# A decoder trunk on one core: index scores in fewer places and ahead of the memory attention, the starting norms in thirds, other places for the top eights

## The reference, cut to what matters

```python
h = layer_norm(x, ln0_g, ln0_b)
for l in range(DEPTH):                       # DEPTH = 2
    pr = split_projection(h @ w_in[l])
    # A: sparse attention on the 128 keys that an index score picks
    logits = einsum('bqhd,bkd->bqhk', qi, ki)            # 8 index heads of 32
    score = einsum('bqhk,bqh->bqk', relu(logits), wi)    # causal, then top 128
    # B: block attention, C: difference of two softmaxes, then an RMS norm
    # D: latent attention, E: attention over 256 rows of mem
    mk, mv = mem @ w_mem_kv[l]
    o = stack(o_a, o_b, o_c, o_d, o_e) * silu(z)
    out = sum(sigmoid(g) * (o @ w_branch), branches) @ w_out[l]
    h = layer_norm(ALPHA * h + out, ln_g[l], ln_b[l])
```

## Time and profile before

| | us |
|---|---|
| median of 3 runs | 1339.69 (1339.42 to 1339.84) |
| profiled execution | 1343.1 |
| its span, first to last instruction | 1341.5 |
| PE busy / DVE / ACT / POOL in the span | 1307.1 / 707.8 / 662.8 / 663.4 |
| mean granted clock of PE | 0.995 |

### The profile page before, as it was taken

How to read it: one execution, slowest core, us unless ns; L and a number is a source line. 1 busy time by engine, 2 the same in 40 slices (tenths; PEclk the granted TensorE clock), 3 DMA queues, 4 the chain that set the end, 5 groups by cost and what they waited for, 6 DMA issues and landing times.

```text
span 1341.5 us, 18893 instructions
## 1 busy us (share of the span) xinstructions
PE 1307.1 (97%) x6744; PEld 1108.3 (83%) x6744; DVE 707.8 (53%) x1700; ACT 662.8 (49%) x1326; POOL 663.4 (49%) x838
## 2 busy tenths in 40 slices
PE   6999999999999999999999999999999999999996
PEld 5888888888888998888887888888888889888885
DVE  4746686554347464513355577675534664454135
ACT  3555445365477475523235552554646665654232
POOL 3443453354565454467435335434445553645774
PEclk8999999999999999999999999999999999999998
DMA  7322232132332143242413223322223213323321
GB/s 278 105 79 64 83 98 79 50 94 64 87 98 59 45 120 109 59 112 77 137 42 109 79 64 92 97 60 73 83 63 103 71 52 88 101 60 92 92 91 63
DMA packets 147053, 116.47 MB, mean 87 GB/s; under 512 B 5520, under 2 KB 131856, under 8 KB 146704
## 3 DMA queue, kind: packets, MB, share of 16 engines
q1 hardware_dynamic: 146816, 114.22, 28.9%
q10 hardware_dynamic: 144, 1.05, 0.2%
HBM read 112.10 MB, written 3.15 MB: 86 GB/s over the span
## 4 chain that ended last, share of the span: by engine, by line
PE 80%; DVE 12%; ACT 4%; issue 2%; DMA 1%; SPq 0%; DVEq 0%; ACTq 0%
PE product L811 19%; PE product L813 18%; PE product L812 18%; PE scores L1036 3%; PE context L1083 3%; PE transposed L1049 3%; PE branch_product L811 3%; PE branch_product L812 3%; PE branch_product L813 3%; PE context L1066 2%; ACT score_operands L1107 1%; DVE index_scores L1568 1%; PE product L911 1%; DVE top_eight L1574 1%; DMA merged<-in_w_mem_kv_dram 1%
## 5 line engine op out<-in xcount | busy, mean ns | idle before, releaser
L795 POOL TENSOR_TENSOR weights_rest<-raw_weights,weights_head 128x320 fp32r<-128x320 f32 (+3 forms) x672 | 542.5, 838 | 391.4 <-ACT weights_head L1107 391.2
L811 PE MATMUL product<-weights_head,stationary_head 128*128 128x512 f32 (+3 forms) x768 | 290.7, 379 | 3.0 <-issue 2.1
L813 PE MATMUL product<-weights_head,stationary_rest 128*128 128x512 f32 (+3 forms) x768 | 284.6, 371 | 0.0
L812 PE MATMUL product<-weights_rest,stationary_head 128*128 128x512 f32 (+3 forms) x768 | 284.5, 370 | 0.0
L1107 ACT ACTIVATE weights_head<-raw_weights 128x1280 fp32r<-128x1280 f32 (+4 forms) x178 | 197.7, 1113 | 142.1 <-PE product L813 116.5
L811 PE MATMUL product<-stationary_head,weights_head 128*128 128x512 f32 x640 | 260.4, 407 | 0.0
L813 PE MATMUL product<-stationary_head,weights_rest 128*128 128x512 f32 x640 | 250.4, 391 | 0.0
L812 PE MATMUL product<-stationary_rest,weights_head 128*128 128x512 f32 x640 | 250.3, 391 | 0.0
L780 POOL TENSOR_TENSOR merged<-merged,activated 128x256 f32<-128x256 f32 x128 | 94.0, 756 | 242.5 <-DVE activated L1712 242.5
L811 PEld LDWEIGHTS product<-weights_head,stationary_head 128*128 128x128 f32 x768 | 144.7, 188 | 25.5 <-issue 3.0
L813 PEld LDWEIGHTS product<-weights_head,stationary_rest 128*128 128x128 f32 x768 | 144.5, 188 | 23.8
(11 more groups left out here) (232 smaller groups left out, 1879.1 us busy)
## 6 DMA issues: line engine op xcount, KB each, us to landing
raw_weights<-in_w_in_dram SPq DMA_DIRECT2D x104, 512.0 KB, 3.7
raw_weights<-in_w_in_dram SPq DMA_DIRECT2D x72, 256.0 KB, 2.9
raw_weights<-in_w_branch_dram SPq DMA_DIRECT2D x80, 128.0 KB, 3.7
raw_weights<-in_w_out_dram SPq DMA_DIRECT2D x16, 512.0 KB, 3.7
merged<-in_w_mem_kv_dram SPq DMA_DIRECT2D x8, 512.0 KB, 7.2
raw_weights<-in_w_in_dram SPq DMA_DIRECT2D x8, 416.0 KB, 3.1
raw_weights<-in_w_in_dram SPq DMA_DIRECT2D x8, 296.0 KB, 4.6
residual<-in_x_dram SPq DMA_DIRECT2D x4, 512.0 KB, 11.5
```

The lines of the kernel that those rows point to most:

```text
L795: ins = nc.gpsimd.tensor_tensor(WL[:, sw, part], RAW[:, sr, part], WH[:, sw, part].bitcast(F32), ALU.subtract)
L811: nc.tensor.matmul(dst, sh, mh, start=start, stop=False)
L812: nc.tensor.matmul(dst, sh, ml, start=False, stop=False)
L813: return nc.tensor.matmul(dst, sl, mh, start=False, stop=stop)
```

## The change

Five things are changed.

1. The start of layer 0. `ln0` comes in three parts that are placed one by one. The loads of the memory weights come earlier and those of tiles 2 and 3 later. The copy of the transposed memory to DRAM is issued at `ek` and not at once. The first memory products wait for one quarter of the transposed memory at a time. `mv` stands ahead of `xj 1`. POOL's bias of tile t is written at its own gain and not one step later.
2. The IX groups. `xj 3` follows (IX,2,2) in place of (IX,2,1), group (IX,2,2) stands ahead of (IX,0,3), and `ek` is written at (IX,0,3), ahead of the split of (IX,3).
3. Index scores take 22 slots in place of 32. E's attention starts four slots later and ends where it did. The top eights of tile 1 start three slots earlier and end three earlier, those of tile 2 start four earlier and end one earlier. B's and D's attention start one slot later each.
4. `DU` uses banks G2 and G3 for tile 2, and S and O for tile 3.
5. C's `fin` is one unit of attention later for heads 0 to 2. The gain of tile 1 at the layer's end (`l2 1`) follows (O1,3,2) in place of (O1,2,2).

```diff
@@ diff_steps
             if (i - 3) % NT == NT - 1:
                 first.append(("fo", "C", (i - 3) // NT))
-                second.append(("fin", "C", (i - 3) // NT))
+        if i >= 7 and i % NT == 3 or i == UNITS + 2:
+            second.append(("fin", "C", (i - 4) // NT if i % NT == 3 else NH - 1))
@@ PLACES
-    ("index transposes", ("E", 0, 2), ("E", 2, 1), 0.0),
-    ("E queries", ("A1", 0, 0), ("A1", 2, 0), 0.0),
-    ("E attention", ("A1", 2, 0), ("B1", 1, 2), 0.0),
-    ("index scores", ("E", 2, 2), ("A0", 2, 1), 0.0),
+    ("index transposes", ("E", 0, 3), ("E", 2, 1), 0.0),
+    ("E queries", ("A1", 1, 0), ("A1", 3, 0), 0.0),
+    ("E attention", ("A1", 3, 0), ("B1", 1, 2), 0.0),
+    ("index scores", ("E", 2, 2), ("A1", 3, 3), 0.0),
...
-    ("B attention", ("gE0", 0, 4), ("gE1", 3, 3), 0.0),
+    ("B attention", ("gE0", 1, 0), ("gE1", 3, 3), 0.0),
@@ plan
-    start = [("ln0", 0), ("ln0", 1), ("ez",), ("mkv", 0), ("ln0", 2), ("xj", 0, 0), ("xj", 0, 1), splits[0], splits[1], ("ln0", 3),
-             ("mkv", 1), ("xj", 1, 0), ("xj", 1, 1), ("mv",), splits[2], ("ln0", 4)]
-    extra[at[(ORDER[0], 1, 1)]] += [("xj", 2, 0), ("xj", 2, 1)]
-    extra[at[(ORDER[0], 2, 1)]] += [("xj", 3, 0), ("xj", 3, 1)]
-    extra[at[(ORDER[0], 2, 2)]].append(("ek",))
+    start = [("ln0", 0, part) for part in ("sums", "scale", "gain")]
+    start += [("ln0", 1, "sums"), splits[0], ("ln0", 1, "scale"), ("ln0", 1, "gain"), ("mkv", 0), ("xj", 0, 0), ("xj", 0, 1), ("ez",),
+              splits[1], ("ln0", 2, "sums"), ("ln0", 2, "scale"), ("ln0", 3, "sums"), ("ln0", 2, "gain"), ("mkv", 1), ("mv",),
+              ("xj", 1, 0), ("xj", 1, 1), ("ln0", 3, "scale"), splits[2]]
+    extra[at[(ORDER[0], 1, 1)]] += [("xj", 2, 0), ("xj", 2, 1), ("ln0", 3, "gain")]
+    extra[at[(ORDER[0], 2, 2)]] += [("xj", 3, 0), ("xj", 3, 1)]
+    extra[at[(ORDER[0], 0, 3)]].append(("ek",))
...
-    extra[at[("O1", 2, 2)]].append(("l2", 1))
+    extra[at[("O1", 3, 2)]].append(("l2", 1))
@@ DMA queue of SP
             load_mk(0, 0)
+            load_mk(0, 1)
             sp.dma_start(LN_IN[:, 0:D], ln0_g.partition_broadcast(P)).then_inc(first_ln_in.sem, first_ln_in.step(("first", 0), 16))
+            sp.dma_start(LN_IN[:, D:2 * D], ln0_b.partition_broadcast(P)).then_inc(first_lb_in.sem, first_lb_in.step(("first", 1), 16))
             load_x(1)
...
+                    if L == 0 and i == 1:
+                        load_mk(0, 2)
+                        load_mk(0, 3)
                     if L == 0 and i == 2:
+                        load_x(2)
                         load_x(3)
@@ banks of DU
+        def du_banks(t):
+            return {1: (("U", U), ("TP", TP)), 2: (("G2", G[2]), ("G3", G[3]))}.get(t, (("S", S), ("O", O)))
```

More of the change, by code:

```diff
@@ L258, in plan @@
         if c == "IX":
-            order = [(0, 0), (1, 0), (0, 1), (1, 1), (2, 0), (2, 1), (0, 2), (1, 2), (0, 3), (2, 2), (1, 3), (2, 3)] + [(3, t) for t in range(NT)]
+            order = [(0, 0), (1, 0), (0, 1), (1, 1), (2, 0), (2, 1), (0, 2), (1, 2), (2, 2), (0, 3), (1, 3), (2, 3)] + [(3, t) for t in range(NT)]
         elif c == "O1":
@@ L485, in build @@
         first_ln_in = tally("first_norm_loaded")
+        first_lb_in = tally("first_norm_bias_loaded")
         ln_in = tally("layer_norm_loaded")
@@ L758, in _ @@
                 for step in PLAN:
-                    if step[0] == "ln0" and L == 0 and 0 < step[1] <= BIASED:
-                        offset(0, step[1] - 1, ("first", step[1] - 1), LN_IN[:, D:2 * D], gained0, normed0)
+                    if step[0] == "ln0" and L == 0 and step[2] == "gain" and step[1] < BIASED:
+                        pool.wait_ge(first_lb_in.sem, first_lb_in.at(0, ("first", 1)))
+                        offset(0, step[1], ("first", step[1]), LN_IN[:, D:2 * D], gained0, normed0)
                     if step[0] == "l2" and step[1] < BIASED:
@@ L895, in _ @@
                         if kh == 0:
[L896 to L901, removed]
+                            claim("U")
+                            claim("S")
+                            if L > 0:
                                 pe.wait_ge(memt_in.sem, memt_in.at(0, ("first",)))
@@ L905, in _ @@
                             if k % 2 == 0:
+                                if L == 0:
+                                    pe.wait_ge(moved.sem, moved.at(0, ("first", kk // 2)))
                                 pe.wait_ge(mk_in[kk // 2].sem, mk_in[kk // 2].at(L, ("mk",)))
@@ L909, in _ @@
                                                  start=kk == 0, stop=kk == KD - 1)
+                            if kk == 0:
+                                claim("G0")
+                                claim("G1")
                             for j in range(2):
@@ L1123, in _ @@
                 copy(MEMT[:, 2 * j:2 * j + 2, :], G[j][:].rearrange("p (k n) -> p k n", k=2)).then_inc(moved.sem, moved.step(("first", j)))
-            act.wait_ge(moved.sem, moved.at(0, ("first", 3)))
-            act.dma_start(SPILL.rearrange("p (k n) -> p k n", k=KD), MEMT).then_inc(spilled.sem, spilled.step(("first",), 16))
             for L in range(DEPTH):
@@ L1136, in _ @@
                         copy(WH[:, w_slot(L, item), 0:n], RAW[:, raw_slot(item), 0:n]).then_inc(head.sem, head.step(step))
-                    elif kind == "ln0" and L == 0 and step[1] < NT:
+                    elif kind == "ln0" and L == 0 and step[2] == "sums":
                         t = step[1]
@@ L1141, in _ @@
                                              bias=CN[:, C_EPS:C_EPS + 1]).then_inc(rooted0.sem, rooted0.step(("first", t)))
-                        if t < NT - 1:
-                            normalize(0, t, ("first", t), summed0, scaled0)
-                    elif step == ("ln0", NT) and L == 0:
-                        normalize(0, NT - 1, ("first", NT - 1), summed0, scaled0)
+                    elif kind == "ln0" and L == 0 and step[2] == "scale":
+                        normalize(0, step[1], ("first", step[1]), summed0, scaled0)
                     elif kind == "l1":
@@ L1153, in _ @@
                     elif kind == "ek":
+                        if L == 0:
+                            act.wait_ge(moved.sem, moved.at(0, ("first", 3)))
+                            act.dma_start(SPILL.rearrange("p (k n) -> p k n", k=KD), MEMT).then_inc(spilled.sem, spilled.step(("first",), 16))
                         for j in range(NH):
@@ L1387, in _ @@
                     if kind == "ln0":
-                        t = step[1]
-                        if L == 0 and t < NT:
+                        t, part = step[1:]
+                        if L > 0:
+                            continue
+                        if part == "sums":
                             dve.wait_ge(x_in[t].sem, x_in[t].at(0, ("first", t)))
```

30 lines of the change are left out of this document (13 added, 17 removed), and 6 rows, old and new, of the table PLACES.

## The result

| | before | after |
|---|---|---|
| median, us | 1339.75 (5 runs, 1339.42 to 1342.49) | 1345.62 (5 runs, 1344.55 to 1346.94) |
| ratio | | 1.0041, 95% interval 1.003 to 1.0052 |
| profiled execution / its span | 1343.1 / 1341.5 | 1344.55 / 1342.9 |

The change makes the kernel 0.4% slower. The forecast was 1336.2, with a range up to 1342. 1.45 + 3.4 + 1.07 is the 5.9 between the medians. Why the first gap exists is part of the answer; the second stays open.

A forecast was written before the change was run, and what follows sets the result against it. PE's work plus its stops was taken to bound the kernel. Layer 0 at -2.85, layer 1 at +0.15 and the end summed to -3.5 us, taken off the median to give 1336.2, range 1331 to 1342.

The forecast's parts named there:

- The likeliest case: Whole kernel: the parts add up as worked out, -3.5 us to 1336.2, own range 1334 to 1338.5, chance 0.42.
- D's start, part 4: D's attention one slot later: ACT's tanh stands ahead of D's copies, +0.1 us per layer (-0.4 to +0.3).
- A hole of over 1 us at any other place: Sign in the changed profile: a PE stop over 1 us outside the places listed makes the prediction wrong.
- its 2.85 us of clock: Start of layer 0: 16 memory matmuls at clock 0.55 take 6.30 us; running at full clock saves 2.85 us.
- Index scores, part 3: Denser index scores: bank U waits for ACT's ReLU, stops sum to 3.7, less DVE's old stops: +2.3 us per layer.
- The rival named "slower": Dense stretch: the ReLU bounds PE throughout, eight more stops of 0.45 us per layer, +7.2 to 1343.4; chance 0.14.
- Start and IX, parts 1 and 2: Start and IX groups up to (IX,3,0): -1.2 us in layer 0 (-5.9 to +0.5), +1.8 in layer 1.
- E's start, part 2: Behind IX: earlier `ek` shrinks one stop by 0.6 and ends 0.4 at E's first group, -1.0 us per layer.
- B, DU, `fin`, the end, parts 4 to 6: Stops removed: B's rotation -0.85, DU's banks -1.0, C's mask behind `fin` -1.2 us per layer; DVE's end -0.8 once.
- The clock: IX stage: a new 1.9 us stop drops the clock, about 7 us of work at half pace, +1.8 to 1338.0; chance 0.07.

The follow-up runs named there:

- the second profile of before: The kernel before, unchanged, profiled once more against its own first profile: this execution took 1339.77 us.
- ix_back: The changed kernel with D's attention, index scores with E's attention and top eights, and the IX stage with `ek` placed as before: 1330.97 us.
- zero_late: Against the changed kernel: D, scores and IX order as before, `ek` kept early; in layer 0's start zeroing moved later, third split earlier: 1329.14 us.
- before_d_late: The kernel before with only D's attention one slot later: 1345.23 us, ratio 1.0039 to before.

## Why the prediction was wrong

The likeliest case was the sum of part after part, -3.5. The traces show +1.45. By its steps:

- **D's start, part 4: +0.1 per layer. The failed step.** The prediction looked at ACT's tanh, ahead of D's copies, and never at DVE, where the rests landed behind a gating that waits for PE. By the traces it cost 3.7 and 2.1, by the runs 5.5 to 6.2 in all, and 4.3 on the kernel before. "A hole of over 1 us at any other place" was named as what would make the prediction wrong, and this is it. With D alone put back the time is 1339.45: inside the range, though still 3.2 above the forecast.
- **From the profile to the median.** I took the sum, with its 2.85 us of clock, off a median that has no such loss. The profiled execution stood 3.4 above the median, and the prediction gave this number without asking what it was. It was for the most part the very row (clock 0.55) that was counted as a gain; the second profile of before, 3.3 shorter, shows it. This would have been wrong with D right, too.
- **Index scores, part 3: +2.3, measured +3.2 per layer.** The mechanism is right, the size short by the stop of 1.0 behind split and table load. The pairs (0.63 and 0.85 for 0.8 and 1.0), A1's unit (1.17 and 0.94 for 1.1 and 0.8) and what DVE gives back (1.6 for 1.47) came nearly as worked out. The rival named "slower" had the place, but with eight stops of 0.45; it was one of 1.0.
- **Start and IX, parts 1 and 2: -1.2 and +1.8.** Measured -2.3 at (IX,3,0) (43.84, where the sum had 44.9, because the chain of the start is 1.1 quicker) and +1.8 in layer 1. Part of the -2.3 is the lost clock of the first profile: against the second one (IX,3,0) comes 0.3 later. That under the new start the old order of IX would gain only 1.05 in layer 0, because tile 3's gain is late, was not in the sum.
- **E's start, part 2: -1.0.** Measured -0.4 ahead of E's first group and -0.9 at the `ek` work, together -1.3. With IX and `ek` put back (`ix_back`, layer 1) both came again.
- **B, DU, `fin`, the end, parts 4 to 6:** -0.85, -1.0, -1.2 and -0.8; measured -0.97, -1.1, -1.42 and -1.0.
- **The clock.** The rival feared it behind the 1.9 us stop in the start, where no trace shows it. It fell behind the stop of 2.3 at D, in one layer of each of two traces, and in `zero_late` behind the 2.4 at tile 3's gain. The "about 7 us" at half pace that the rival counted with have only the window of 6.3 us of rows 3 beside them; the falls at D and in `zero_late` cost 1.6 and 1.2.

The section on the change has the top eights of tile 1 start three slots earlier; by the diff and the plan it is two. Nothing in the sum rests on it.

The miss of 9.4 is 5.0 by which the traces differ from the sum, 3.4 between profile and median of before and 1.07 between median and profile of after. Of the 5.0, D is 5.6 and the scores 1.9; the start, E's start and the small gains, each a little better than forecast, take 2.5 back.

## What to carry to other kernels

When a list of small steps is moved by one slot, look at every engine's neighbours in the new slots, not at the one engine that was busy there before. A short instruction that frees a bank costs whatever stands ahead of it on its own engine, and the worst to have there is one that waits for PE in the same slot. And before a sum made on one trace is taken off a median, find out what in the trace makes that execution differ from the median; a stretch at half clock is the first suspect.

## What the runs showed of the hardware

- Each fall of the clock in these traces ahead of a kernel's end stands behind a stop of PE, but a stop of the same size did not always bring one. By the idle time as printed: 2.14 at D was followed by 0.57 in layer 0 and 1.00 in layer 1 of the changed kernel, and by 1.00 in layer 0 and a fall in layer 1 of `before_d_late`; 2.17 by 1.00 and 3.83 by 0.55 in the two profiles of before; 2.43 by 0.50 in `zero_late`. The Trainium skill ("TensorE: Matmul & The Clock Gate", section "What's actually happening") has the clock set by how busy PE has been recently. The rows agree for the longest stop, and show that between 2.1 and 2.4 us it can go either way.
- The first tanh of a layer costs a table load of 1.28 us on ACT. The Trainium skill ("ScalarE: Activation LUTs", section "What ACT_TABLE_LOAD costs") gives 1283 ns, which the trace has to the digit, and 1380 ns more for a drain; here the tanh starts 1.29 us after the load does, and the load 0.02 us after the split's end, so no drain is seen.
